# VectorE adds and clips the third block of an up pair ahead of the pair-after-next's first weight sum

## What is computed

```
def sqrelu_mlp(h, w_up, w_down):
    return jnp.square(jax.nn.relu(h @ w_up)) @ w_down

xp = xp + sqrelu_mlp(rms_norm(xp, mlp_norm_g[i]), mlp_w_up[i], mlp_w_down[i])
xs = xs + sqrelu_mlp(rms_norm(xs, mlp_norm_g[i]), mlp_w_up[i], mlp_w_down[i])
```

## Time and profile before

| | |
|---|---|
| median of 3 runs | 1485.1 us (1484.34 to 1486.83) |
| the profiled execution's own time | 1487.48 us |
| its span, first to last instruction | 1485.7 us |
| TensorE matmul busy | 1430.1 us, 96% |
| VectorE, ScalarE, GpSimd busy | 66%, 48%, 57% |
| mean granted TensorE clock | 0.986 |

### The profile page before, as it was taken

The page is one execution under the profiler, slowest core; times in us unless marked ns, Lnnn a source line. Parts: engine busy times, 40 slices in busy tenths (PEclk is TensorE's granted clock), DMA queues, the critical chain, the costliest instruction groups (busy, mean ns, idle before and its releaser), DMA issues.

```text
span 1485.7 us, 29349 instructions
## 1 busy us (share of the span) xinstructions
PE 1430.1 (96%) x10168; PEld 1342.7 (90%) x10168; DVE 980.1 (66%) x1787; ACT 715.4 (48%) x1506; POOL 847.8 (57%) x634
## 2 busy tenths in 40 slices
PE   9999999998899899998999999999988998999989
PEld 7889999998899899998988778787988998999989
DVE  5006716777767767667777676867777677676674
ACT  4323101135636546455537586765356364464552
POOL 8454455444766657667786052351447667576674
PEclk9999999999999999999999999999999999999999
DMA  7222232211232222222343010101102322222222
GB/s 253 92 77 70 91 104 71 71 56 34 90 105 87 86 85 85 85 85 85 133 132 90 30 43 15 42 30 41 57 30 86 103 94 78 96 85 85 85 85 92
DMA packets 36541, 120.46 MB, mean 81 GB/s; under 512 B 6056, under 2 KB 6760, under 8 KB 36208
## 3 DMA queue, kind: packets, MB, share of 16 engines
q1 hardware_dynamic: 32320, 111.83, 22.6%
q10 hardware_dynamic: 4144, 7.65, 1.6%
HBM read 115.91 MB, written 3.55 MB: 80 GB/s over the span
## 4 chain that ended last, share of the span: by engine, by line
PE 50%; POOL 21%; issue 18%; DVE 6%; ACT 3%; DMA 2%; POOLq 0%; SPq 0%; DVEq 0%; ACTq 0%
POOL w_lo L751 18%; PE ps L865 8%; PE ps L867 8%; PE ps L866 8%; PE ps L1032 5%; PE ps L1034 5%; PE ps L1033 5%; POOL op_lo L757 3%; PE ps L1392 2%; DMA raw<-stream 2%; PE ps L1209 2%; PE ps L1332 1%; PE ps L1007 1%; PE ps L1335 1%; PE ps L974 1%
## 5 line engine op out<-in xcount | busy, mean ns | idle before, releaser
L751 POOL TENSOR_TENSOR w_lo<-raw,w_hi 128x512 fp32r<-128x512 f32 x256 | 349.3, 1375 | 208.3 <-ACT w_hi L2199 207.6
L1032 PE MATMUL ps<-op_hi,w_hi 128*128 128x288 f32 x896 | 271.5, 303 | 28.4 <-POOL op_lo L757 28.4
L1033 PE MATMUL ps<-op_lo,w_hi 128*128 128x288 f32 x896 | 269.4, 301 | 0.0
L1034 PE MATMUL ps<-op_hi,w_lo 128*128 128x288 f32 x896 | 268.6, 300 | 0.0
L715 POOL TENSOR_SCALAR w_hi<-raw 128x1024 fp32r<-128x1024 f32 x75 | 83.2, 1109 | 271.5 <-PE ps L867 120.5
L2199 ACT CAST w_hi<-raw 128x512 fp32r<-128x512 f32 x256 | 158.5, 620 | 118.7 <-PE ps L1034 118.3
L1032 PEld LDWEIGHTS ps<-op_hi,w_hi 128*128 128x128 f32 x896 | 173.3, 193 | 30.2 <-POOL op_lo L757 30.2
L717 POOL TENSOR_TENSOR w_lo<-raw,w_hi 128x1024 fp32r<-128x1024 f32 x75 | 186.5, 2487 | 6.3
L1034 PEld LDWEIGHTS ps<-op_hi,w_lo 128*128 128x128 f32 x896 | 173.6, 194 | 0.0
L1033 PEld LDWEIGHTS ps<-op_lo,w_hi 128*128 128x128 f32 x896 | 173.4, 194 | 0.0
L1032 PE MATMUL ps<-x_hi_four,w_hi 128*128 128x288 f32 x512 | 152.3, 297 | 2.1 <-DVE ps L1711 2.1
(11 more groups left out here) (252 smaller groups left out, 3838.1 us busy)
## 6 DMA issues: line engine op xcount, KB each, us to landing
raw<-stream SPq DMA_DIRECT2D x207, 512.0 KB, 3.5
x<-xt SPq DMA_DIRECT2D x8, 288.0 KB, 7.2
out_x<-x ACTq DMA_DIRECT2D x8, 288.0 KB, 2.1
b_bc<-bs ACTq DMA_DIRECT2D x2, 512.0 KB, 6.4
cache_raw<-cache_ct ACTq DMA_DIRECT2D x1, 1024.0 KB, 5.6
v_out<-sgu_grow ACTq DMA_DIRECT2D x1, 512.0 KB, 5.3
ws_sb<-ws ACTq DMA_DIRECT2D x2, 256.0 KB, 4.9
out_v<-v_out ACTq DMA_DIRECT2D x1, 512.0 KB, 4.3
```

Of the source, the lines that this page charges most:

```text
L751: nc.gpsimd.tensor_tensor(block_of(w_lo, f), factor(n, f), block_of(w_hi, f).bitcast(F32), ALU.subtract).then_inc(w_low_set, 1)
L1032: nc.tensor.matmul(out, l_hi, r_hi, start=first, stop=False, skip_group_check=True)
L1033: nc.tensor.matmul(out, l_hi, r_lo, start=False, stop=False, skip_group_check=True)
L1034: done = nc.tensor.matmul(out, l_lo, r_hi, start=False, stop=last, skip_group_check=True)
```

## The change

In the up pairs' stream of VectorE one call moves two places down: `first_sums(..., 0)` of pair n+2 now comes behind `add_c22` and `clip_c22` of pair n, and so directly ahead of its part 1. Nothing else differs; the counts that others wait for are those of before. There are 32 up pairs (2 MLPs, 4 quarters, 4 pairs).

```
                         add_u4(q, n)
                         low_sum(mlp, q, n + 1, S2)
-                        first_sums(mlp, q, n + 2, unit0, 0)
                         add_c22(q, n)
                         clip_c22(q, n)
+                        first_sums(mlp, q, n + 2, unit0, 0)
                         first_sums(mlp, q, n + 2, unit0, 1)
                         clip_banks(q, n)
```

## The result

The changed kernel takes 1458.11 us in the median (1457.89 to 1459.60, 4 runs) against 1485.39 before; the ratio is 0.9818, with a 95% interval of 0.9801 to 0.9835.

The account below looks back on a forecast made before the run. TensorE, busy 96%, was bound by waits on late engines. Gains of 9.3 + 8.8 = 18.1 us gave 1469.4 from the profiled 1487.48; for the median, 1485.1 - 16.9 = 1468.2 us, own range 1464 to 1473, range 1461 to 1478.

Parts of the forecast that it names:

- the chain: Last up pair of a quarter: transfer, L1602, add, clip, square, cast S4, GpSimd's S4, GpSimd's L757, TensorE.
- both waits: TensorE's waits in the up pairs: eight for GpSimd's L757, 28.4 us, and thirteen for ScalarE's copy, 12.3 us.
- The square was to start 2.4 us earlier: ScalarE's square in a quarter's last up pair: may start 2.38 us earlier, of which 1.01 us reaches GpSimd.
- a wait of 2.4 us: TensorE's wait for L757, once per quarter: some 2.4 us stays where 3.40 is shown, 19 us in all.
- The eleven waits for the copy: TensorE's waits for ScalarE's copy, without the two opening an MLP: all go, 7.05 + 11 x 0.16 = 8.8 us.
- the two gains: In the up pairs, 9.3 us on GpSimd and 8.8 us on ScalarE's copy, said to add up.
- the step on TensorE's clock: Lower clock behind TensorE's eight L757 waits: all stretches stay, gain 0; were they to go, 8 x 1.6 = 13 us more.
- the clock stretches go as well: Rival: of the lower-clock stretches behind TensorE's L757 waits, half go, 1462 us, or all, 1455; chance 0.09.
- L1602 against GpSimd: VectorE's L1602 overlapping GpSimd: meets the same A12 and S3, taken as nothing; otherwise 3.7 us lost or gained.
- The slower rival: L1602 and L1606 in one run delay `clip_banks` and the copy, if L1602 takes 1.9 to 2.2 us; 1489, chance 0.04.
- It moves no transfer: Weight transfers that L1602 waits for: the change leaves them in place, so L1602 starts about where it did.
- L1602's waits for transfers were to stay: Sign in the profile after: VectorE's L1602 still waits for transfers; before, 24 such waits took 33.5 us.

Follow-up runs that it names:

- half: Kernel before, with L1602 moved only between the add and the clip of the third block; 1475.65 us, ratio 0.9917.
- ready_data: Kernel before, old order, with the moved sum reading a constant table, so only its second part waits for the transfer; 1459.94 us, ratio 0.9816.
- last_pair: Kernel before, with the changed order in the last up pair of each quarter alone; 1470.40 us, ratio 0.9882.
- first_pairs: Kernel before, with the changed order in the first three up pairs of each quarter, the old one in the last; 1476.56 us, ratio 0.9919.
- detuned kernels: Changed kernel with 6, 12 or 26 more TensorE matmuls ahead of pair 0's A11, quarters 1 to 3, both MLPs; 1465.68, 1477.17, 1479.78 us.
- hidden_first: Changed kernel, with GpSimd making the low part of the last up pair's squares ahead of factor S4's; 1444.77 us, ratio 0.9727 to before.
- before12: Kernel before, with 12 more TensorE matmuls ahead of pair 0's A11 in quarters 1 to 3 of both MLPs; 1497.95 us, ratio 1.0060.

## Why the prediction was wrong

**Right: the chain and both waits.** The transfer held the clip only by VectorE's order (half, ready_data). The square was to start 2.4 us earlier (2.29 measured, 3.81 less 1.52), of which 1.01 reach GpSimd, and a wait of 2.4 us was to be left, 19 in all: 2.36 and 18.9 measured. The eleven waits for the copy are gone. The waits gave 18.4 us in the profiled execution against 18.1 predicted. That the two gains are separate is shown by last_pair and first_pairs.

**Wrong: the step on TensorE's clock,** "I leave all eight stretches in, gain 0". Six of the eight went, and one in the opening of the first MLP, which the prediction had not put in question; the remainder of the sum is 11.3 us. The step took the length of the wait as what decides and looked for the nearest row (2.69 us, followed by the low level). The row itself does not hold: the same wait, 2.67 us after the change, is followed by the full clock. The detuned kernels show that the same 2.36 us is or is not followed by the low level according to the moment: 7 of 8 against 2 of 8. So for a wait of this length the outcome was open, and nothing in the change aims at it: that six went was luck. The six fall alike. In the changed kernel three end at 494.14, 586.34 and 678.54 and three at 1224.42, 1316.61 and 1408.81, 92.2 us apart in either MLP, and all are spared; that it is the even spacing that spares them together is likely but not shown. The price of a stretch, 1.6 us, was right. The rival "the clock stretches go as well", at 1455 to 1462, is what happened, with 0.09 given to it. The range stopped at 1461 and left most of it out; a term that can be worth 0 or 13 us and hangs on a moment that no row of before fixes belonged in the range with both its ends. The waits alone give the predicted 1468.2, 10 us above the measured time.

**The other terms.** L1602 against GpSimd was taken as nothing, and in the pair shown it is: GpSimd's A12 and S3 take 3.01 us, 3.00 before. The slower rival needed L1602 above 1.9 us; its maximum stayed at 1.79. "It moves no transfer" was wrong, and with it one sign in the profile: L1602's waits for transfers were to stay, and they fell to 1.8 us, since VectorE comes later and the transfer some 0.4 us earlier. It cost the sum nothing: no wait of TensorE stands behind L1602 now.

**Open.** What the moment is measured against is shown by no row here, so none of the 2 of 8, 4 of 8 and 7 of 8 could have been foretold from the rows of before. The Trainium skill, "TensorE: Matmul & The Clock Gate", section "What's actually happening", says that the clock is judged over a window that runs freely and does not restart with the kernel. The detuned kernels agree with that, but do not prove it. It was not tried whether VectorE's order matters for the opening waits (2.7 and 2.6 us), which every kernel kept.

## What to carry to other kernels

In an engine's hand-written order, put what waits for a transfer behind what is ready and has others waiting for it; look for it where an engine idles for a DMA and another idles for that engine. When a wait of TensorE gets shorter, count the lower clock behind it as a separate term with two ends, and give both to the range. If work recurs with a fixed period, the clock can fall behind nearly all of its waits or behind few of them, so a small change elsewhere in the period can gain or lose ten microseconds by that alone.

## What was not expected of the hardware

Adding 26 matmuls in six places cost 21.7 us, adding 12 cost 19.1: more work, nearly the same time, as the low clock behind the same 2.36 us waits came and went. The waits of 1.13 us in hidden_first were followed by the full clock in all eight cases, but so was one of 3.33 us in before12 and one of 3.40 in first_pairs (it ends at 1334.35). A wait of 1.47 us in each opening, shortly behind the one of 2.7, was followed by the lower level in every kernel; clock 0.54 from 353.97 to 357.17 in the changed one.
